# Shorter low-part products in the experts' 64-row tiles, and the output gate product in three passes

## What is computed

```python
def moe(hn, router_w, router_b, w_gu, b_gu, w_down, b_down):
    ...
    gu = lax.ragged_dot(xs, w_gu, group_sizes) + b_gu[sorted_e]
    gate = jnp.minimum(gu[:, ::2], SWIGLU_LIMIT)
    up = jnp.clip(gu[:, 1::2], -SWIGLU_LIMIT, SWIGLU_LIMIT)
    act = (up + 1.0) * (gate * jax.nn.sigmoid(SWIGLU_ALPHA * gate))
    y = lax.ragged_dot(act.astype(w_down.dtype), w_down, group_sizes) + b_down[sorted_e]
...
def second_block(...):
    ...
        ssm = jax.nn.gelu(ssm)
        ssm = ssm * jax.nn.sigmoid(ssm @ w_glu[l] + b_glu[l])
        ssm = _rms_norm(ssm, ssm_out_g[l]) * jax.nn.silu(g_ssm)
        mixed = jnp.concatenate([attn, ssm], axis=-1) @ w_out[l]
        x = x + _rms_norm(mixed, post_norm_g[l])
```

## Time and profile before

| | us |
|---|---|
| median of 3 runs | 5543.3 |
| lowest and highest | 5541.6 and 5545.59 |
| the profiled execution | 5537.53 |
| span of its trace | 5535.9 |

### The profile page before, as it was taken

The page is one execution under the profiler, slowest core; times in us unless marked ns, Lnnn a source line. Parts: engine busy times, 40 slices in busy tenths (PEclk is TensorE's granted clock), DMA queues, the critical chain, the costliest instruction groups (busy, mean ns, idle before and its releaser), DMA issues. The chain is left out here.

```text
span 5535.9 us, 78003 instructions
## 1 busy us (share of the span) xinstructions
PE 5178.5 (94%) x25453; PEld 3527.3 (64%) x25454; DVE 3221.1 (58%) x6021; ACT 2176.3 (39%) x3294; POOL 633.3 (11%) x865
## 2 busy tenths in 40 slices
PE   7999996899999999999999999799996599999698
PEld 4666664566666666666666666455554488888365
DVE  5444444667676777777777777644343544444166
ACT  4222221444444445555555555222223533333154
POOL 0000000000000000000000000101000299300000
PEclk9999997899999999999999999899998799999899
DMA  8777774656556567777777776522322300000533
GB/s 287 232 258 227 251 238 144 218 163 191 179 173 196 161 201 235 235 235 235 235 235 235 235 235 216 176 99 102 110 98 87 105 5 9 7 7 7 181 113 104
DMA packets 432864, 921.87 MB, mean 167 GB/s; under 512 B 62960, under 2 KB 87984, under 8 KB 432048
## 3 DMA queue, kind: packets, MB, share of 16 engines
q1 hardware_dynamic: 372208, 758.67, 42.2%
q10 hardware_dynamic: 33216, 87.05, 4.9%
q0 software_dynamic: 27280, 74.02, 4.1%
HBM read 774.11 MB, written 147.59 MB: 166 GB/s over the span
## 5 line engine op out<-in xcount | busy, mean ns | idle before, releaser
L1260 DVE TENSOR_TENSOR w_lo_gate<-stage,w_hi 128x1024 bf16<-128x1024 f32 (+1 forms) x800 | 929.8, 1179 | 188.1 <-ACT w_hi L1129 131.0
L1129 ACT ACTIVATE w_hi<-stage 128x1024 fp32r<-128x1024 f32 (+1 forms) x800 | 791.5, 1017 | 577.9 <-PE GU L950 297.9
L947 PE MATMUL GU<-w_hi,x_hl 128*128 128x512 f32 x2048 | 859.2, 420 | 17.7 <-DVE x_hl L1265 7.6
L948 PE MATMUL GU<-w_hi,x_hl 128*128 128x512 f32 x2048 | 810.8, 396 | 0.0
L950 PE MATMUL GU<-w_lo_gate,x_bf 128*128 128x512 bf16 x2048 | 499.4, 382 | 0.0
L947 PEld LDWEIGHTS GU<-w_hi,x_hl 128*128 128x128 f32 x2048 | 386.0, 188 | 133.6 <-issue 27.4
L947 PE MATMUL Y<-w_hi,a_hl 128*128 128x512 f32 x1024 | 456.7, 446 | 1.7 <-DVE a_hl L1271 1.7
L948 PEld LDWEIGHTS GU<-w_hi,x_hl 128*128 128x128 f32 x2048 | 387.0, 189 | 82.7
L948 PE MATMUL Y<-w_hi,a_hl 128*128 128x512 f32 x1024 | 404.4, 395 | 0.0
L950 PEld LDWEIGHTS GU<-w_lo_gate,x_bf 128*128 128x128 bf16 x2048 | 174.9, 98 | 255.4 <-issue 89.9
L2672 DVE TENSOR_REDUCE ntop<-SC 128x1 f32<-128x2048 f32 x64 | 146.7, 2292 | 269.8 <-PE SC L2781 269.8
(11 more groups left out here) (613 smaller groups left out, 9274.3 us busy)
## 6 DMA issues: line engine op xcount, KB each, us to landing
stage<-in_expert_w_gate_up_dram SPq DMA_DIRECT2D x512, 512.0 KB, 5.1
stage<-in_expert_w_down_dram SPq DMA_DIRECT2D x224, 512.0 KB, 6.2
mixer_stage<-w_in_lo SPq DMA_DIRECT2D x150, 512.0 KB
mixer_stage<-in_w_out_dram SPq DMA_DIRECT2D x65, 512.0 KB, 9.3
expert_rows<-zero_y SPq DMA_DIRECT2D x64, 512.0 KB
mixer_stage<-w_out_rows SPq DMA_DIRECT2D x64, 512.0 KB
b_gu<-in_expert_b_gate_up_dram ACTq DMA_DIRECT2D x128, 256.0 KB, 4.7
expert_rows<-acted ACTq DMA_DIRECT2D x64, 512.0 KB, 3.0
```

The lines of the kernel that those rows point to most:

```text
L947: pe.matmul(out, high(k), w_high(k), start=(k == first), stop=False)
L948: pe.matmul(out, low(k), w_high(k), start=False, stop=False)
L1129: act.activation(w_hi[:, c, ks, :], staged, ACT.Copy).then_inc(s["hi_done"], 1)
L1260: dve.tensor_tensor(w_lo[:, c, ks, :], staged, w_hi[:, c, ks, :], ALU.subtract).then_inc(s["lo_done"], 1)
```

## The change

In short tiles, the bf16 product takes 64 columns as its stationary operand and writes 64 partitions; the zeros, their two VectorE instructions per tile and the semaphore `bf_zeroed` go. The bf16 matmuls now stand ahead of the last `both` matmul, since the one that closes the accumulation writes all 128 partitions. In the output phase, the gate product is written out: four matmuls with `g_hi` after a wait for `g_hi_ready`, then the wait for `gT_sb`, four with `g_lo` and four with `g_bf`.

```diff
             def mid(i, t, g):
-                dve.wait_ge(s["x_ready"], g * 2 + 2)
-                dve.memset(x_bf[:, :, HALF:P], 0.0)
-                dve.memset(a_bf[:, :, HALF:P], 0.0).then_inc(s["bf_zeroed"], 1)
                 plain(i, g, HALF)
...
+                def both(k):
+                    columns = hl[:, k, :, :].rearrange("p h c -> p (h c)")[:, n:n + P]
+                    return pe.matmul(out, columns, w_hi[:, c, k, :], start=(k == 0), stop=(k == KD - 1))
+
+                for k in ks[:-1]:
+                    both(k)
                 for k in ks:
-                    both = hl[:, k, :, :].rearrange("p h c -> p (h c)")[:, n:n + P]
-                    pe.matmul(out, both, w_hi[:, c, k, :], start=(k == 0), stop=False)
-                pe.wait_ge(s["bf_zeroed"], g + 1)
-                for k in ks:
-                    mm = pe.matmul(out, bf[:, k, :], w_lo[:, c, k, :], start=False, stop=(k == KD - 1))
-                return mm
+                    pe.matmul(out[0:n], bf[:, k, 0:n], w_lo[:, c, k, :], start=False, stop=False)
+                return both(ks[-1])
...
                 if has_this:
                     if is_step(t, 0):
                         pe.wait_ge(s["w_low"], 1)
-                    pe.wait_ge(s["gT_sb"], t * 2 + 2)
+                    pe.wait_ge(s["g_hi_ready"], t + 1)
                     if has_prev:
                         pe.wait_ge(s["pre_ready"], t)
-                    split_product(pe, GL[:, :], lambda k: g_hi[:, k, :], lambda k: g_lo[:, k, :], lambda k: g_bf[:, k, :],
-                                  lambda k: glu(w_hi)[:, k, :], lambda k: glu(w_lo)[:, k, :], range(KS), 0, KS - 1).then_inc(s["gl_ps"], 1)
+                    for k in range(KS):
+                        pe.matmul(GL[:, :], g_hi[:, k, :], glu(w_hi)[:, k, :], start=(k == 0), stop=False)
+                    pe.wait_ge(s["gT_sb"], t * 2 + 2)
+                    for k in range(KS):
+                        pe.matmul(GL[:, :], g_lo[:, k, :], glu(w_hi)[:, k, :], start=False, stop=False)
+                    for k in range(KS):
+                        mm = pe.matmul(GL[:, :], g_bf[:, k, :], glu(w_lo)[:, k, :], start=False, stop=(k == KS - 1))
+                    mm.then_inc(s["gl_ps"], 1)
```

More of the change, by code:

```diff
@@ L995, in expert_phase @@
         Y = pb("Y2", 2 * BANK)
-        names = """ident_ready bf_zeroed rows_free ids_free ids_seen xT_ps x_hi_ready x_ready bg_in0 bg_in1 bg_in2
+        names = """ident_ready rows_free ids_free ids_seen xT_ps x_hi_ready x_ready bg_in0 bg_in1 bg_in2
             bg_in3 bd_in hi_done lo_done gu_ps gu_taken gate_ready tanh_ready acted_ready aT_ps a_hi_ready a_ready y_ps y_taken
@@ L1309, in first @@
             def first(i, g):
-                dve.sem_inc(s["bf_zeroed"], 1)
                 low(i, 14)
```

## The result

The changed kernel takes 5558.7 us (median of 10 runs, 5555.0 to 5564.3) against 5542.4 us (10 runs, 5535.8 to 5545.6) for the kernel before: a ratio of 1.0033 with an interval of 1.0024 to 1.0041, slower by a third of a per cent. The forecast was 5561.0 us. It stood on a median of 5543.3 us from three executions of the kernel before; the ten executions above have 5542.4, so that +16.3 us were measured where +17.7 were forecast. The span of its trace grew from 5535.9 to 5553.3 us, by 17.4.

What follows compares the result with a forecast made beforehand. TensorE was taken to set the pace of the expert phase; -12.1 (wait) + 32.4 (shape changes) - 2.6 (output phase) = +17.7 us on the 5543.3 us median gave 5561.0 us, range 5545 to 5571, 66 in 100.

Steps and rivals of the forecast that it cites:

- The wait that goes: Chunk 0 of each short tile: TensorE no longer waits for `bf_zeroed`, 0.98 us in the first; 12.1 us gained over 12 tiles.
- The price of a call: Each call of `product` in short tiles: changing to 64 columns 0.10 us and back 0.19, together 0.30 (0.17 to 0.39).
- the nine open calls: Nine of a short tile's 11 `product` calls, with no wait to cover their cost: 12 x 9 x 0.30 = 32.4 us lost.
- the two foreign places, lines 2329 and 832: Shape changes elsewhere in the earlier trace, 128*64 and 64*128 to 128*128: 0.09 us lost at each.
- Two calls under cover: Last two calls of a short tile: their 2 x 0.30 us fit in the 0.80 us wait on `x_lo`, costing nothing.
- The short tiles together: The 12 short tiles: 12.1 us gained from the wait on `bf_zeroed`, 32.4 us lost to changes of shape.
- The output phase: Gate product in three passes: nothing in tiles 3 to 15, 2.6 us gained (2.3 to 3.1) in tiles 0 to 2.
- the price of tile 1: Output phase, tile 1: four `g_hi` matmuls come free, 4 x 0.23 to 4 x 0.43 us; 1.2 taken as gain.
- That the change of shape costs nothing: Rival, short tiles: the array switches without emptying; -14.7 us, 5528.6 us; 14 in 100.
- only the emptying: Rival, short tiles: the load lies beside the emptying, 0.17 us per call; sum +3.7, 5547.0 us; 10 in 100.
- That `OUT` is not held by `o_n`: Rival, output phase: gate product gives 0.65 us in each of 13 tiles; sum +9.2, 5552.5 us; 6 in 100.
- That narrow loads don't get beside the matmuls: Rival, nine calls of a short tile: 35 64-column loads lose over 0.03 us each; +13 us or more, 5574; 4 in 100.

Runs made afterwards that it cites:

- the three runs of the output phase: Against the kernel before: gate product in three passes alone, `o_n` ahead of `g_lo` alone, and both; 16.01, 15.79 and 15.09 us per output tile.

## Why the prediction was right

**The wait that goes** (12.1 us). Right: from the last wide matmul to the first narrow one are 0.32 us instead of 1.22, and nothing else waits at that place.

**The price of a call** (0.30 us). The mechanism and the size were right. Between the starts of wide matmuls of neighbouring chunks it is 3.91 - 3.59 = 0.32. Over the nine open calls, from the tile's start to the transposes `TX`, it is less. They started 1057.71 - 1035.86 = 21.85 us into the tile before:

```profile
1057.71 1.04 PE L1480 MATMUL TX<-ident,rows 128*128 128x128 f32 x8
```

and start 1061.17 - 1037.58 = 23.59 into it now: 1.74 = 9 x 0.302 - 0.98. It splits as the prediction put it, by the unrounded starts: the first narrow matmul 0.320 behind the last wide one (0.230 and 0.09, which the prediction reads as the array's emptying), the second 0.240 behind the first (0.216 and 0.024 for the open load of 64 columns, for which 0.03 was assumed without a row), the wide one 0.309 behind the last narrow one (0.216 and 0.09), and the one behind that 0.338 (0.230 and 0.108). So the two foreign places, lines 2329 and 832, gave the price of a change that the trace of before did not contain. That the 0.09 us are an emptying is a reading: the runs show the longer distance at the changes of shape, and not what the array does in it. The prediction's lower bound has a slip: twice 0.09 less 0.02 is 0.16 and not 0.17, which moves the lower end of its range by 1 us.

The estimate of 0.32 from the formula of the Trainium skill's "TensorE: Matmul & The Clock Gate", section LDWEIGHTS, was no better: a load of 64 bf16 columns is shown as 0.106 to 0.110 us, twice the 0.053 of that formula, and nearly all of it is hidden. The rule of the Trainium skill's "TensorEngine Tiling (Array Packing)", section Key Properties, that changing the tiling mode drains TensorE, agrees with the starts in both directions, 0.09 us each.

**Two calls under cover** (0). Right: the tile's end moves as `TX` does, by 1.74 us, and 0.19 us of cover are left where 0.20 was expected.

**The short tiles together**: +20.3 was the sum, +20.5 measured. Both of its terms stand. One reading behind them was loose: two of the slices of the earlier trace rows with short tiles show 8 tenths and not 9 or more. It does no harm, since the short tile itself has a granted clock of 1.00 in both traces, as a stretch.

**The output phase.** Tiles 3 to 15 at nothing: right, with 16.0 us per tile and the idle time where it was expected, and the experiment with `o_n` ahead shows the reason: once `o_n` is out of the way, the same edit gives 15.79 - 15.09 = 0.70 us per tile, which is what the prediction said `GL` gains. Tiles 0 to 2 at 2.6 us: this term was too large for this trace; 1.9 were measured (0.5, 0.7 and 0.7). TensorE's waits there, against the earlier trace rows:

```profile
PE GL L3317 <- DVE w_lo L3275: 9.8, 1, 9.8
PE GL L3317 <- ACT g_hi L3130: 4.2, 1, 4.2
...
PE GL L3320 <- DVE g_lo L3199: 1.9, 1, 1.9
```

What was mis-sized is the price of tile 1. `OUT` does start earlier there, 18.29 us into the tile instead of 19.78, so 1.5 us and more than the 1.2 put down. But from there to the next tile it takes 11.93 us instead of 11.13. In the kernel before, the clock was back at its full level when these 48 matmuls began (1.00 over all of them); now the first 1.7 us of them lie in the stretch at half clock (1.2 GHz). The two rows are of the changed kernel and of the one with two changes per call, which has the same output phase (length, busy times, and the granted clock behind POOL):

```profile
5291.77:5293.47 1.70, 1.70 (x6) 1.32 (x5) 1.10 (x2) 0.38 (x1) 0.00 (x0) 0.50 0.00 0
```
```profile
5322.76:5333.70 10.94, 10.94 (x50) 7.44 (x49) 7.14 (x20) 3.63 (x7) 0.00 (x0) 1.00 0.30 96
```

How much is handed back differs from execution to execution. In all eight kernels with the gate product in three passes `OUT` starts 18.1 to 18.3 us into tile 1; in the second row's kernel the clock is back before it, and the tile takes 29.2 us, and in the other seven 30.2 to 30.8, against 30.9 before. So the gain in tile 1 is 0.1 to 1.7 us, and the forecast's 1.2 and the trace's 0.7 both lie in that. A gain ahead of a slow stretch can be handed back inside it.

**What was not in the sum.** 1.2 us came at the end of the program: the stretch at half clock in the last tile's output product is shorter in this trace. Before and after, with the granted clock in the column behind POOL:

```profile
5512.70:5518.70 6.00, 6.00 (x14) 4.75 (x15) 5.48 (x15) 0.00 (x0) 0.00 (x0) 0.50 0.50 175
```
```profile
5532.30:5535.90 3.60, 3.60 (x10) 2.80 (x9) 3.18 (x14) 0.00 (x0) 0.00 (x0) 0.53 0.68 237
```

This too is not fixed by one trace. From the last tile's first `OUT` matmul to the end are 23.2 and 23.1 us in the two kernels with the old gate product, and 20.4 to 22.0 in the eight with the new one; in three of these the whole product runs at full clock. Over tiles 0 to 2 and the last tile together, the six kernels that have the new gate product and the old place of `o_n` gain 2.9 to 3.6 us. That is a steadier figure than its parts, and the fair one to set beside the forecast's 2.6.

So the ledger of the span is: +17.7 forecast, +0.2 in the short tiles, +0.7 in tiles 0 to 2, -1.2 at the end, +1.7 before and in the first expert tile, and -1.6 in the rest, which makes 17.5 for the 17.4 measured. The last two are of the execution and not of the change, and that they nearly cancel is luck: the sum agrees with the span better than its single terms do.

**The rivals.** That the change of shape costs nothing, or only the emptying, is out by the starts and by the experiment with twice the changes (+2.21 us for 7 pairs). That `OUT` is not held by `o_n` is out by the three runs of the output phase: the gate product alone leaves the tile at 16.0 us, and with `o_n` out of the way it gives 0.7. That narrow loads don't get beside the matmuls is out too: narrow matmuls in a call stand 0.216 us apart from the second on.

## What to carry to other kernels

In these runs halving a matmul's stationary columns saved nothing in its slot and cost a change of shape on each side, some 0.30 us per run of narrow matmuls. It paid when the free half of the array was given the next matmul of the run. The runs should be few and long: at 0.216 us saved per pair, a run needs four narrow matmuls or more (an estimate from these two figures). And where two waits end within 0.2 us of each other, test the removal of both: here each alone was worth 0 and 0.2 us per tile, and together 0.9.

When a kernel's list of waits becomes empty and its time grows, read the starts: distances between neighbouring matmuls show costs that are booked as busy time.

## What the runs showed of the hardware

- Two bf16 matmuls with 64 stationary columns each, on different column halves, both adding into the same PSUM bank under an open accumulation of 128-wide fp32r matmuls, run side by side: eight in 0.98 us from the first to the next wide one, against 1.85 one behind the other. The pairs of line 2329 in the earlier trace rows had shown this for separate results only.
- At full clock a change of shape between 128*128 fp32r and 128*64 bf16 lengthens the distance between starts by 0.09 us in either direction. The distance behind it is longer too, by what is loaded: 0.024 us for 64 bf16 columns, 0.108 for 128 fp32r ones (read here as the part of the load that lies open).
- A load of 64 bf16 columns is recorded at 0.106 to 0.110 us, and yet hides in a slot of 0.216 and in pairs.
- In tile 1 of the output phase, an output product that began 1.5 us earlier ended only 0.7 earlier, since its first 1.7 us lay at half clock. Over all eight kernels with the gate product in three passes the gain of the tile was 0.1 to 1.7 us, by when the clock came back. What brings it back wasn't tried.
